# Nine subtractions of the recurrent inputs move from VectorE to GpSimd

## The reference

```
p_shift = p_shift + mu_shift * (token_shift(p_shift) - p_shift)
pr, pk, pv, pw, pa, pg = split(p_shift)            # 3 x 768, 64, 64, 128 columns
wf = w0 + tanh(pw) @ w2;  decay = exp(-exp(-softplus(-wf) - 0.5))
a = sigmoid(a0 + pa @ a2)
kk = heads(pk * k_k);  kk = kk / max(norm(kk), 1e-12)
k = pk * (1 + (a - 1) * k_a)
bonus = sum(rf * heads(k) * r_k) * vf
```

## Time and profile before

| | |
|---|---|
| median of 3 runs | 3331.85 us (3330.82 to 3332.04) |
| the profiled execution | 3327.23 us, its span 3325.4 us |
| mean granted TensorE clock | 0.928 of full speed |
| PE busy | 2887.2 us, 87% of the span |
| DVE busy | 1992.2 us, 60% |
| ACT busy | 1418.9 us, 43% |
| POOL busy | 212.2 us, 6% |
| the stage of the recurrent inputs | 2156.48 to 2331.34 us of the span, 174.86 us |

### The profile page before, as it was taken

The page is one execution under the profiler, slowest core; times in us unless marked ns, Lnnn a source line. Parts: engine busy times, 40 slices in busy tenths (PEclk is TensorE's granted clock), DMA queues, the critical chain, the costliest instruction groups (busy, mean ns, idle before and its releaser), DMA issues. The chain is left out here.

```text
span 3325.4 us, 39502 instructions
## 1 busy us (share of the span) xinstructions
PE 2887.2 (87%) x15396; PEld 2340.4 (70%) x15396; DVE 1992.2 (60%) x1990; ACT 1418.9 (43%) x1383; POOL 212.2 (6%) x179
## 2 busy tenths in 40 slices
PE   7977777599999999999996498796899759789997
PEld 6637757488888888888884484564899647668876
DVE  4454432799999999999996443367443363332223
ACT  3222331377777777777773322244222212232222
POOL 0000300000000000000001000000354100000000
PEclk9988898699999999999998799798999879989998
DMA  4222302489999999999997223110000212222220
GB/s 173 94 102 96 109 27 86 171 344 382 372 377 383 378 370 384 382 365 382 384 374 266 95 100 124 58 65 10 12 2 1 82 67 90 85 76 90 101 80 34
DMA packets 111505, 596.26 MB, mean 179 GB/s; under 512 B 10848, under 2 KB 13536, under 8 KB 64448
## 3 DMA queue, kind: packets, MB, share of 16 engines
q1 hardware_dynamic: 92032, 533.07, 41.5%
q10 hardware_dynamic: 12304, 35.89, 2.9%
q0 software_dynamic: 7056, 25.69, 2.3%
HBM read 569.44 MB, written 25.17 MB: 179 GB/s over the span
## 5 line engine op out<-in xcount | busy, mean ns | idle before, releaser
L1320 DVE TENSOR_TENSOR weights_low<-weight_ring,weights_high 128x2048 fp32r<-128x2048 f32 x384 | 865.9, 2288 | 70.5 <-ACT weights_high L1267 67.5
L1267 ACT CAST weights_high<-weight_ring 128x2048 fp32r<-128x2048 f32 x384 | 722.8, 1906 | 217.2 <-PE psum L1191 147.6
L362 DVE TENSOR_TENSOR w_low<-weight_ring,w_high 128x2048 fp32r<-128x2048 f32 (+1 forms) x96 | 225.4, 2348 | 353.5 <-ACT w_high L357 343.8
L357 ACT CAST w_high<-weight_ring 128x2048 fp32r<-128x2048 f32 (+1 forms) x87 | 164.5, 1891 | 320.1 <-PE psum L389 163.0
L1191 PE MATMUL psum<-weights_high,expert_x_high 128*128 128x512 f32 x1024 | 278.9, 394 | 2.8 <-DVE expert_x_low L1324 2.8
L1191 PE MATMUL psum<-weights_low,expert_x_high 128*128 128x512 f32 x1024 | 275.4, 391 | 0.0
L1191 PE MATMUL psum<-weights_high,expert_x_low 128*128 128x512 f32 x1024 | 274.0, 389 | 0.0
L1191 PEld LDWEIGHTS psum<-weights_low,expert_x_high 128*128 128x128 f32 x1024 | 193.4, 189 | 40.9
L1191 PEld LDWEIGHTS psum<-weights_high,expert_x_low 128*128 128x128 f32 x1024 | 192.6, 188 | 40.2
L1191 PEld LDWEIGHTS psum<-weights_high,expert_x_high 128*128 128x128 f32 x1024 | 190.9, 189 | 41.1 <-DVE expert_x_low L1324 3.2
L389 PE MATMUL psum<-mix_hT_high,w_high 128*128 128x512 f32 x384 | 158.5, 413 | 12.9 <-PEq L224 9.4
(11 more groups left out here) (470 smaller groups left out, 5321.2 us busy)
## 6 DMA issues: line engine op xcount, KB each, us to landing
weight_ring<-in_w_gu SPq DMA_DIRECT2D x256, 1024.0 KB, 8.5
weight_ring<-in_w_down SPq DMA_DIRECT2D x128, 1024.0 KB, 8.7
weight_ring<-in_w_in SPq DMA_DIRECT2D x35, 1024.0 KB, 4.9
weight_ring<-in_w_ada SPq DMA_DIRECT2D x24, 1024.0 KB, 4.8
weight_ring<-in_w_ffn_in SPq DMA_DIRECT2D x22, 1024.0 KB, 4.8
expert_table<-expert_y ACTq DMA_DIRECT2D x32, 512.0 KB, 8.7
weight_ring<-in_w_ffn_out SPq DMA_DIRECT2D x11, 1024.0 KB, 4.8
weight_ring<-in_w_out SPq DMA_DIRECT2D x8, 1024.0 KB, 4.8
```

The costliest lines, as they stand in the source:

```text
L357: self.m.nc.scalar.copy(high, w).then_inc(self.rounded.sem, 1)
L362: self.m.nc.vector.tensor_tensor(low, w, high.bitcast(F32), ALU.subtract).then_inc(self.ready.sem, 1)
L1267: nc.scalar.copy(high[:, n % 4, :], slot(n)).then_inc(rounded.sem, 1)
L1320: V.tensor_tensor(low[:, n % 4, :], slot(n), high[:, n % 4, :].bitcast(F32), ALU.subtract).then_inc(ready.sem, 1)
```

## The change

`Split.rest` can now be given an engine other than VectorE. In `rwkv_inputs` a new GpSimd list makes the low parts of units 1 to 9, one after another, each as soon as ScalarE has rounded the unit; VectorE's list loses the same nine operations. Buffers, semaphores and all other stages stay.

```diff
-    def rest(self, dve, i):
+    def rest(self, eng, i, ops=None):
         u, w, high, low = self.parts_of(i)
-        dve.wait_ge(self.rounded.sem, self.rounded.at(i + 1))
-        self.m.nc.vector.tensor_tensor(low, w, high.bitcast(F32), ALU.subtract).then_inc(self.ready.sem, 1)
+        eng.wait_ge(self.rounded.sem, self.rounded.at(i + 1))
+        (ops or self.m.nc.vector).tensor_tensor(low, w, high.bitcast(F32), ALU.subtract).then_inc(self.ready.sem, 1)
...
+        @block.gpsimd
+        def _(pool):
+            for u in range(1, N // 2):
+                split.rest(pool, u, nc.gpsimd)
+
         @block.vector
...
             for i in range(N):
                 j, q = (i - 2) // 3, (i - 2) % 3
-                if i % 2 == 0 and i < N - 2:
-                    split.rest(dve, i // 2 + 1)
                 shift(i)
```

## The result

The change takes 3340.74 us (median of 6 runs, 3334.8 to 3348.77) against 3331.34 us of the kernel before (6 runs, 3326.94 to 3334.84). The ratio is 1.0032, with a 95% interval of 1.0017 to 1.0047: 0.3% slower, or 10.7 us with 5.7 to 15.7; the two medians lie 9.4 us apart. The forecast was +10.6 us and 3342.5 us.

The account below looks back on a forecast made before the run. Bound by a loop over TensorE, ScalarE and VectorE: shifts 4.2, L2005 4.4, clock 1.8 and unit 3 0.2 sum to +10.6 us, removal's 2.4 us included; 3331.85 + 10.6 = 3342.5 us, range 3336.5 to 3348.0.

Parts of the forecast that it names:

- The loop and its four units: Loop over TensorE, ScalarE, VectorE: units 5 and 8 delay the shift 2.1 us each, 4 and 7 delay L2005 2.2 each.
- VectorE stands still while GpSimd reads: Shift and L2005, with two SBUF inputs, wait for GpSimd's end; blocked rows longer than 0.7 us, ending 0.7 us behind it.
- GpSimd's own time: One 128x2048 float32 subtraction on GpSimd takes 4.3 us, forecast between 4.0 and 4.7 us.
- Unit 3: Shift of tile 4 is 0.7 us late behind GpSimd; a ScalarE table load covers most: +0.2 us.
- The clock: Behind unit 4, TensorE's wait grows to 3.9 us and its clock falls to 1.2 GHz: +1.8 us.
- Stage and total: Stage grows from 174.9 to some 185.5 us, total by 10.6 us to 3342.5 us.
- Free running: Rival: GpSimd and VectorE work side by side, leaving only the removal's 2.4 us gain: 3329.5 us; chance 0.12.
- The quick GpSimd: Rival: GpSimd's subtraction takes 3.1 us, adding 3.8 to 5.6 us: about 3336.5 us; chance 0.08.
- the slow one: Rival: GpSimd's subtraction takes 5.3 us, adding 15.6 us: 3347.5 us; chance 0.08.
- The reciprocal: Rival: at units 4 and 7 GpSimd waits for VectorE's reciprocal, making L2005 4.3 us late: 3346.6 us; chance 0.05.
- TensorE waited for no low part: Answers a rival: GpSimd late for TensorE beyond unit 2's 7.3 us, costing at most 1 or 2 us; chance 0.02.

Follow-up runs that it names:

- the reordered kernel: Kernel before, all low parts on VectorE, but units 5 and 8 rounded behind the root and subtracted behind L2009: 3323.25 us against 3330.03 us, ratio 0.998.

## Why the prediction was right

- **The loop and its four units.** Right, and shown by doing the parts alone: +7.0 us for units 4 and 7, +5.8 for 5 and 8, +0.2 for the five others.
- **VectorE stands still while GpSimd reads.** Right. All the rows named in the forecast are long (3.10, 4.71, 3.08 and 4.71 us); twice the work blocks twice. One detail was off: a blocked operation ends 0.54 us behind GpSimd, not 0.7. The words "fully blocks", which the prediction quotes from the Trainium skill (SBUF — State Buffer, Who interferes with whom), stand there beside VectorE's two-port modes; for two inputs in SBUF the section says that they contend with GpSimd's reading.
- **GpSimd's own time.** Mis-sized: 4.3 us assumed, 4.53 to 4.61 us measured where nothing held it up. It made each of the four waits about 0.2 us longer: +9.3 in place of 8.6 us for the four. The Trainium skill's 4497 ns (GPSIMD Engine Reference, Performance versus the Vector engine) was nearer than my line through two rows.
- **Unit 3.** +0.2 us forecast, +0.2 us measured alone.
- **The clock.** Right for unit 4 (1.8 us forecast, 1.6 us measured), but I charged it there only. Where TensorE already fell to 1.2 GHz before, it stayed there longer behind units 7 and 8, 0.8 us each, and 0.1 us behind unit 5 (0.3 and 0.5 us in two other profiles). I had taken the four old values from 8.25 to 8.79 us as a fixed price of a wait.
- **Stage and total.** The stage grew by 12.8 us where 10.6 was forecast; the difference is 1.5 us of clock and some 0.7 us of GpSimd's time. In the total the 10.7 us of the ratio (5.7 to 15.7) can't tell these apart, and that it lies within 0.1 us of the forecast is luck.
- **The rivals.** Free running is out, and its price was wrong as well: 0.8 us, not 2.4 us, since the clock took the rest back. The quick GpSimd (3.1 us) and the slow one (5.3 us) are out, since it took 4.6 us. The reciprocal did not hold GpSimd back: its operation began at 2190.65 inside the reciprocal (2189.28 to 2192.63) and took 4.57 us. TensorE waited for no low part.

Between the sums and the copy of the v tile TensorE was at the low clock for 3.4 us (unit 4 after the change) to 6.8 us (unit 5 in the reordered kernel). Part of this is settled: how much of a low stretch falls on work depends on whether it begins in the wait, as in the kernel before, or behind the sums, as in the reordered one (2229.1 against 2228.65). What sets its beginning no run here shows, and it stays open: the same wait of 2.87 us was followed by 1.2 GHz in one kernel and by 2.4 GHz in the other. That the 6.8 us by which the last version is faster exceed the 4.4 to 4.8 us of its stage lies within the interval.

## What to carry to other kernels

Work moved from VectorE to GpSimd is not hidden just because GpSimd is idle: ask for each moved operation which VectorE operation with two inputs in SBUF falls into its time, and whether that one is on the path. Here 20.6 us were taken off VectorE, of which 2.4 us lay on the path (0.8 us once the clock had taken its share), and four blocks were put on it that cost 2.3 us each even net of that. Moving the work behind the row that releases the waiting engine, on the same engine, gained what the second engine could not: 3.0 us of the stage by itself. Where a change moves the waits of TensorE, look at the granted clock behind every one of them, those that were left alone too.

## What the runs showed of the hardware that was not expected

- GpSimd's filling of 128x2048 float32 took 1.8 us, its copy 1.9 us, its subtraction, with two inputs, 4.6 us: 2.7 us more than the copy, which is more than the copy's whole time.
- GpSimd that only writes leaves two-input operations of VectorE alone but holds up its TENSOR_SCALAR in SBUF (1.59 in place of 0.42 us).
- A shorter wait of TensorE (4.67 in place of 5.51 us) was followed by more work at 1.2 GHz (5.9 in place of 4.5 us): the 6.8 us at the low clock were the same, but less of them lay in the wait. And one wait of 2.87 us was followed by 1.2 GHz in one kernel and by 2.4 GHz in another.
- The same program reached this stage at times between 2150.1 and 2161.2 us, while the stage's length repeated to 0.4 us. An effect of a few microseconds is better read from its stage than from the total.
